# Stick-breaking attention: sums over later keys as fp32r products of a high and a low part, three units per head pair in place of four

## The reference, cut to what matters

```python
z = jnp.einsum('bhqd,bhkd->bhqk', q_blk, kt).astype(jnp.float32) * scale
mask = key_pos[None, :] < q_pos[:, None]
log_not = jnp.where(mask, jax.nn.log_sigmoid(-z), 0.0)
between = lax.cumsum(log_not, axis=3, reverse=True) - log_not
a = jnp.where(mask, jnp.exp(jax.nn.log_sigmoid(z) + between), 0.0)
return jnp.einsum('bhqk,bhkd->bhqd', a.astype(vt.dtype), vt)
```

## Time and profile before

| | |
|---|---|
| median of 3 runs | 2131.18 us (2130.68 to 2132.56) |
| the profiled execution's own time | 2132.41 us |
| its span in the trace | 2130.7 us |
| PE busy | 2027.6 us (95%) |
| DVE, ACT, POOL busy | 1144.8, 858.7, 341.2 us |
| mean granted clock of PE | 0.982 |
| attention stage, first matmul to last copy | 891.5 to 1015.9 us |
| PE, DVE, ACT, POOL busy in 891 to 1012 us | 106.7, 54.8, 68.9, 49.8 us |

### The profile page before, as it was taken

How to read it: one execution, slowest core, us unless ns; L and a number is a source line. 1 busy time by engine, 2 the same in 40 slices (tenths; PEclk the granted TensorE clock), 3 DMA queues, 4 the chain that set the end, 5 groups by cost and what they waited for, 6 DMA issues and landing times. The chain is left out here.

```text
span 2130.7 us, 27982 instructions
## 1 busy us (share of the span) xinstructions
PE 2027.6 (95%) x11430; PEld 1603.4 (75%) x11430; DVE 1144.8 (54%) x1422; ACT 858.7 (40%) x1242; POOL 341.2 (16%) x310
## 2 busy tenths in 40 slices
PE   8999889899988989998999999999999999999998
PEld 5777886577787768744778888877889878888886
DVE  4445537644564753244468547635332967745753
ACT  4246424524543451355345324333123735423432
POOL 1200615120062520144220000022000012000002
PEclk9999989999998999999999999999999999999999
DMA  6211102221111222200222232223322012223221
GB/s 231 73 66 40 42 18 103 106 73 60 40 42 50 71 86 92 100 30 0 79 99 81 93 113 91 83 94 125 112 79 80 1 60 81 98 90 117 98 83 67
DMA packets 30787, 167.64 MB, mean 79 GB/s; under 512 B 2827, under 2 KB 9635, under 8 KB 14916
## 3 DMA queue, kind: packets, MB, share of 16 engines
q1 hardware_dynamic: 30228, 165.07, 22.3%
q10 hardware_dynamic: 432, 0.79, 0.1%
HBM read 159.52 MB, written 10.00 MB: 80 GB/s over the span
## 5 line engine op out<-in xcount | busy, mean ns | idle before, releaser
L305 PE MATMUL psum<-inputs_high,weights_high 128*128 128x512 f32 x928 | 384.4, 414 | 24.3 <-DVE inputs_low L253 16.6
L307 PE MATMUL psum<-inputs_high,weights_low 128*128 128x512 f32 x928 | 368.2, 397 | 0.0
L306 PE MATMUL psum<-inputs_low,weights_high 128*128 128x512 f32 x928 | 367.8, 396 | 0.0
L2098 PE MATMUL psum<-inputs_high,weights_high 128*128 128x512 f32 x704 | 276.2, 392 | 0.5 <-DVE inputs_low L2242 0.5
L2100 PE MATMUL psum<-inputs_high,weights_low 128*128 128x512 f32 x704 | 274.0, 389 | 0.0
L2099 PE MATMUL psum<-inputs_low,weights_high 128*128 128x512 f32 x704 | 274.0, 389 | 0.0
L258 DVE TENSOR_TENSOR weights_low<-weights_raw,weights_high 128x2048 fp32r<-128x2048 f32 x68 | 160.3, 2359 | 190.1 <-ACT weights_high L247 190.0
L305 PEld LDWEIGHTS psum<-inputs_high,weights_high 128*128 128x128 f32 x928 | 176.3, 190 | 82.3 <-DVE inputs_low L253 22.0
L306 PEld LDWEIGHTS psum<-inputs_low,weights_high 128*128 128x128 f32 x928 | 176.8, 190 | 41.5 <-issue 5.3
L247 ACT CAST weights_high<-weights_raw 128x2048 fp32r<-128x2048 f32 x68 | 129.0, 1898 | 195.2 <-PE psum L307 179.8
L307 PEld LDWEIGHTS psum<-inputs_high,weights_low 128*128 128x128 f32 x928 | 176.5, 190 | 40.5
(11 more groups left out here) (384 smaller groups left out, 3220.5 us busy)
## 6 DMA issues: line engine op xcount, KB each, us to landing
weights_raw<-w_stream SPq DMA_DIRECT2D x116, 1024.0 KB, 4.8
weights_raw<-w_down SPq DMA_DIRECT2D x32, 704.0 KB, 4.0
residual_parked<-residual SPq DMA_DIRECT2D x2, 2048.0 KB, 10.1
residual_back<-residual_parked SPq DMA_DIRECT2D x2, 2048.0 KB, 7.8
residual<-x_t SPq DMA_DIRECT2D x2, 1024.0 KB, 7.8
bias_by_row<-bias_rows SPq DMA_DIRECT2D x2, 1024.0 KB
bias_by_row<-bias_rows SPq DMA_DIRECT2D x1, 1536.0 KB
out_t<-residual SPq DMA_DIRECT2D x5, 256.0 KB, 2.4
```

What stands on the lines that cost most here:

```text
L305: pe.matmul(out, hi, self.ahi[:, k], start=start and b == 0, stop=False)
L306: pe.matmul(out, hi, self.alo[:, k], start=False, stop=False)
L307: mm = pe.matmul(out, lo, self.ahi[:, k], start=False, stop=stop and b == blocks - 1)
L2098: pe.matmul(out, wh, hi, start=start, stop=False)
```

## The change

The unit list goes from four to three per pair. Unit n=0 holds key tiles 3 and 2 side by side (128 and 256 queries), n=1 holds tile 1 (384), and n=2 holds tile 0 (512); the widths with both heads are 768, 768 and 1024 columns. POOL no longer keeps a running total: it copies softplus to a high part with fp32r as its result (into the buffer `weights_high`, which is free in this stage), and DVE subtracts to make the low part (into `weights_low`). PE sums anew for each key tile: the triangle over the tile's own high and low parts, and minus ones over the parts of every later tile, with fp32r operands. The table of minus ones and the triangle is copied to fp32r once. DVE's list is now `softplus(u)`, `cap(u+2)`, `low(u)`, and PE's triangle products wait for `low(u)`.

```diff
...
-    negtri, negones = con[:, K_NEGTRI:K_NEGTRI + P], con[:, K_NEGONES:K_NEGONES + P]
-    pairs = SB_HEADS // 2
-    units = [(p, jt) for p in range(pairs) for jt in reversed(range(TT))]
+    pairs, per = SB_HEADS // 2, 3
+    units = [(p, n) for p in range(pairs) for n in range(per)]
...
-    with ExitStack() as stack, phase(nc, "z", "capped", "exp", "log", "softplus", "masked", "later", "sums", "weights",
-                                     "kept", "out", "out_copy", "bias_repeated") as s:
+    width = (3 * P, 3 * P, 4 * P)
+    blocks = (((3, 0, P), (2, P, 3 * P)), ((1, 0, 3 * P),), ((0, 0, 4 * P),))
+    earlier = (((0, 0, P, 2 * P),),
+               ((0, P, 3 * P, P), (0, 0, P, 2 * P)),
+               ((1, 0, 3 * P, P), (0, P, 3 * P, 2 * P), (0, 0, P, 3 * P)))
+    with ExitStack() as stack, phase(nc, "z", "capped", "exp", "log", "softplus", "masked", "high", "low", "sums", "weights",
+                                     "kept", "out", "out_copy", "signs", "bias_repeated") as s:
...
-        later = stack.enter_context(sbuf(nc, "later_keys", [P, 2, 2, T], F32))
...
+        signs = stack.enter_context(sbuf(nc, "minus_ones", [P, 2 * P], F32R))
+        negtri, negones = signs[:, 0:P], signs[:, P:2 * P]
+        parts = [x.rearrange("p u c -> p (u c)") for x in (k.whi, k.wlo)]
...
         def zbank(u):
...
-        def made_later(u):
-            return (TT - 1) * (u // TT) + min(u % TT, TT - 1)
+        def part(x, p, n):
+            first = 2 * 3 * P * (2 * n + p % 2 if n < 2 else 4)
+            return x[:, first:first + 2 * width[n]].rearrange("p (y i) -> p y i", y=2)
...
             @block.tensor
             def _(pe):
                 def scores(u):
-                    p, jt = units[u]
+                    p, n = units[u]
                     if u >= 3:
...
+                    for m, (jt, first, end) in enumerate(blocks[n]):
+                        for y in range(2):
+                            rows = slice(64 * y, 64 * y + 64)
+                            mm = pe.matmul(zbank(u)[:, y, first:end], qk[rows, 8 + p, jt * P:(jt + 1) * P],
+                                           qk[rows, p, jt * P:], start=m == 0, stop=False, skip_group_check=True)
+                    mm.then_inc(s.z, 1)
+                def sums(u):
+                    p, n = units[u]
+                    if n == 0:
+                        pe.wait_ge(s.low, u + 1)
+                    else:
+                        pe.wait_ge(s.softplus, u + 1)
+                    for of, first, end, to in earlier[n]:
+                        for y in range(2):
+                            for x in parts:
+                                pe.matmul(zbank(u)[:, y, to:to + end - first], negones, part(x, p, of)[:, y, first:end],
+                                          start=False, stop=False, skip_group_check=True)
+                    if n:
+                        pe.wait_ge(s.low, u + 1)
                     for y in range(2):
-                        rows = slice(64 * y, 64 * y + 64)
-                        mm = pe.matmul(zbank(u)[:, y, jt * P:], qk[rows, 8 + p, jt * P:(jt + 1) * P],
-                                       qk[rows, p, jt * P:], start=True, stop=False, skip_group_check=True)
-                    mm.then_inc(s.z, 1)
-                def sums(u):
-                    p, jt = units[u]
-                    pe.wait_ge(s.softplus, u + 1)
-                    pe.wait_ge(s.masked, u + 1)
-                    if jt < TT - 1:
-                        pe.wait_ge(s.later, 2 * made_later(u))
-                    for y in range(2):
-                        if jt < TT - 1:
-                            pe.matmul(zbank(u)[:, y, (jt + 1) * P:], negones, later[:, u % 2, y, (jt + 1) * P:],
-                                      start=False, stop=False, skip_group_check=True)
-                        mm = pe.matmul(zbank(u)[:, y, jt * P:], negtri, softp[:, u % 2, y, jt * P:],
+                        pe.matmul(zbank(u)[:, y, 0:width[n]], negtri, part(parts[0], p, n)[:, y],
+                                  start=False, stop=False, skip_group_check=True)
+                        mm = pe.matmul(zbank(u)[:, y, 0:width[n]], negtri, part(parts[1], p, n)[:, y],
...
                 def values(u):
-                    p, jt = units[u]
+                    p, n = units[u]
...
-                    if jt == TT - 1 and p >= 2:
+                    if n == 0 and p >= 2:
...
-                    for y in range(2):
-                        hd = 2 * p + y
-                        mm = pe.matmul(ps[64 * y:64 * y + 64, 6 + p % 2, jt * P:], v[:, jt, hd * 64:hd * 64 + 64],
-                                       w[:, u % 2, y, jt * P:], start=jt == TT - 1, stop=jt == 0,
-                                       skip_group_check=True)
+                    for jt, first, end in blocks[n]:
+                        for y in range(2):
+                            hd = 2 * p + y
+                            mm = pe.matmul(ps[64 * y:64 * y + 64, 6 + p % 2, jt * P:], v[:, jt, hd * 64:hd * 64 + 64],
+                                           w[:, u % 2, y, first:end], start=jt == TT - 1, stop=jt == 0,
+                                           skip_group_check=True)
...
                 for u in range(3):
                     scores(u)
+                pe.wait_ge(s.signs, 1)
                 for u in range(n_units + 1):
                     if u < n_units:
                         sums(u)
...
             @block.vector
             def _(dve):
                 def cap(u):
-                    jt = units[u][1]
+                    n = units[u][1]
...
                     if u >= 3:
...
-                    dve.tensor_scalar(zc[:, u % 3, :, jt * P:], zbank(u)[:, :, jt * P:], 40.0, None, ALU.min) \
+                    dve.tensor_scalar(zc[:, u % 3, :, 0:width[n]], zbank(u)[:, :, 0:width[n]], 40.0, None, ALU.min) \
...
                 def softplus(u):
-                    jt = units[u][1]
+                    n = units[u][1]
...
                     if u >= 2:
-                        dve.wait_ge(s.sums, u - 1)
-                        dve.wait_ge(s.later, 2 * made_later(u - 1))
-                    dve.tensor_tensor(softp[:, u % 2, :, jt * P:], zbank(u)[:, :, jt * P:], zc[:, u % 3, :, jt * P:],
-                                      ALU.max).then_inc(s.softplus, 1)
+                        dve.wait_ge(s.high, u - 1)
+                        dve.wait_ge(s.low, u - 1)
+                    dve.tensor_tensor(softp[:, u % 2, :, 0:width[n]], zbank(u)[:, :, 0:width[n]],
+                                      zc[:, u % 3, :, 0:width[n]], ALU.max).then_inc(s.softplus, 1)
+                def low(u):
+                    p, n = units[u]
+                    dve.wait_ge(s.high, u + 1)
+                    dve.tensor_tensor(part(parts[1], p, n), softp[:, u % 2, :, 0:width[n]],
+                                      part(parts[0], p, n).bitcast(F32), ALU.subtract).then_inc(s.low, 1)
...
                 def copy_out(p):
-                    dve.wait_ge(s.out, TT * (p + 1))
+                    dve.wait_ge(s.out, per * (p + 1))
...
+                dve.tensor_copy(signs[:], con[:, K_NEGTRI:K_NEGTRI + 2 * P]).then_inc(s.signs, 1)
                 cap(0)
                 cap(1)
                 for u in range(n_units):
                     softplus(u)
                     if u + 2 < n_units:
                         cap(u + 2)
-                    if u >= 5 and (u - 5) % TT == 0:
-                        copy_out((u - 5) // TT)
+                    low(u)
+                    if u >= per + 1 and (u - per - 1) % per == 0:
+                        copy_out((u - per - 1) // per)
...
             def _(act):
                 def logs(u):
-                    jt = units[u][1]
-                    z = zc[:, u % 3, :, jt * P:]
+                    z = zc[:, u % 3, :, 0:width[units[u][1]]]
...
                 def weights(u):
-                    jt = units[u][1]
+                    n = units[u][1]
...
                     if u >= 2:
...
-                    act.activation(w[:, u % 2, :, jt * P:], zbank(u)[:, :, jt * P:], ACT.Exp).then_inc(s.weights, 1)
+                    act.activation(w[:, u % 2, :, 0:width[n]], zbank(u)[:, :, 0:width[n]], ACT.Exp).then_inc(s.weights, 1)
                 for u in range(n_units + 1):
                     if u < n_units:
                         logs(u)
...
             @block.gpsimd
             def _(pool):
-                def keep(x, jt):
-                    d = x[:, :, jt * P:(jt + 1) * P]
+                def keep(x, n):
+                    tiles = len(blocks[n])
+                    d = x[:, :, 0:tiles * P].rearrange("p y (b i) -> p y b i", b=tiles)
...
-                                              pattern=[[0, 2], [1, P]], channel_multiplier=-1)
+                                              pattern=[[0, 2], [0, tiles], [1, P]], channel_multiplier=-1)
                 for u in range(n_units + 1):
                     if u < n_units:
```

(20 more changed lines are left out.)

## The result

The changed kernel takes 2151.42 us (median of 4 runs, 2148.96 to 2155.24) against 2131.87 for the one before in the same comparison (median of 4, 2130.68 to 2135.4): 19.5 us more, ratio 1.009 (95% interval 1.0076 to 1.0103). I had forecast 9.6 us more, with a range of 2133 to 2153.

What follows compares the result with a forecast made beforehand. Bound: a ring of sums, weights and scores, PE and ACT taking turns. Seven pairs 4.5 plus start and end 3.1 made 7.6, plus clock 2: +9.6 us, from 2131.2 to 2141; range 2133 to 2153.

Steps and rivals of the forecast that it cites:

- The ring: Attention stage, every unit: low, sums, weights, scores, cap, next low; 15.88 us per pair against 15.24, seven pairs 4.5 us more.
- the narrow products: Four minus-ones products of 128 columns behind low at n = 0: priced 0.84 us; from below 0.116 each, 0.46.
- The parts off the ring: Ones products, softplus and POOL's copy beside the ring: hidden, with only 0.3 us to spare at n = 2.
- Start and end: Attention stage outside its seven pairs of ring: 7.3 and 13.5 us against 17.7 before, 3.1 us more.
- The clock: Half PE speed over one or two units, at the stage's start and end: 2 us more, bounds 0 and 4.
- If PEclk falls in mid-stage: Sign that the prediction is wrong: PE's granted clock falling in the middle of the attention stage; no size given.
- The half-clock rival: Much slower: PE at half clock throughout the attention stage, +40 us, about 2181; chance 0.08.
- the port rival: Slower: DVE and POOL hold each other up, each low waiting for one keep; 1.5 us more per pair, 2153; chance 0.10.
- The faster rival: The old ring still binds, cap and low staying off it: 12.8 us per pair, about 2115; chance 0.06.

Runs made afterwards that it cites:

- Low twice: The changed kernel with every low done twice, one behind the other with a wait between: 2188.2 us, ratio 1.0265 to the kernel before.
- the two other orders of DVE: The changed kernel with DVE's list reordered: low(u) ahead of cap(u+2), 2137.35 us; or cap(u+1) in place of cap(u+2) ahead of low(u), 2118.57 us.
- the filler: The changed kernel plus 8 fp32r products of zeros on PE before the sums of each pair's first unit: 2139.46 us, ratio 1.0032 to the kernel before.
- the orders with low right behind POOL: The changed kernel with low(u) ahead of cap(u+2), 2137.35 us, or with cap(u+1) ahead of low(u), 2118.57 us; in both low waited for POOL's high.
- the order with cap one unit ahead: The changed kernel with DVE's list as softplus(u), cap(u+1), low(u): 2118.57 us, ratio 0.9955 to the kernel before.
- low before cap: The changed kernel with DVE's list as softplus(u), low(u), cap(u+2): 2137.35 us, ratio 1.0023 to the kernel before.

## Why the prediction was right and wrong

*The ring.* Right in place; in size too, but in part by luck, since the price of the narrow products and the rest of the ring were off in opposite ways. 7 pairs at 15.80 instead of 15.24 make 3.9 us; the prediction had 4.5. Low twice and the two other orders of DVE show that it is this order that sets the pace. The parts off the ring were hidden as said (ones, softplus, POOL's copy at 0.82 and 1.04 us).

*The narrow products.* Wrong in the value chosen: they start 0.11 to 0.12 us apart, as the lower bound had it. The Trainium skill, page "TensorE: Matmul & The Clock Gate", section "Back-to-back issue gap", gives about 81 ns at 128 columns; this trace has 110 to 120, so the measurement decides.

*Start and end.* The prediction had 3.1 us more. With the filler it is 131.92 - 7 x 15.80 = 21.3 us instead of 17.7: 3.6. Of this 0.5 us is the first round and the round with the wide low of 1.36, which are longer than 15.80; cut as the prediction cuts it, from the stage's start to the first low's end and from the last pair's first low's end to the end, it is 7.3 and 13.5 us, just as forecast.

*The clock.* This is the step that failed: "I add 2 (bounds 0 and 4)". The clock came to 11.1 us, the difference of the stages with and without filler. The mechanism was named, as half clock after PE's gaps, but placed at the start and the end alone. There the price was about right: 2.9 us in the first round and 0.1 at the end. What failed is that the six rounds between were put at nothing, where the runs showed 8.1 us: five of the six had half clock after the gap of 2.2 us in which PE waits for low. "If PEclk falls in mid-stage" stood among the signs of being wrong, and it did. The half-clock rival was turned down with "no idle stretch in the ring reaches the 4 us" of the earlier trace rows. That argument failed twice. The 4 us were the time between two windows of one gap, which lasted 5.98 us, and not a least length; the gap in the ring is 2.2 us, behind a stretch that PE filled only in part, and half clock followed it in most pairs but not in all (the pair from 950.43 kept 2.4 GHz). And I had set only full speed throughout against half speed throughout, while the case that came lies between: one stretch in most pairs. Stage by parts: 3.9 + 3.6 + 11.1 = 18.6 of 18.65 us. That 2151.42 us still lies inside the range of 2133 to 2153 is luck: the upper end was drawn for the port rival, not for the clock.

The span grew 2 us less than the stage: 0.4 us by an earlier start, and the rest in the output product behind it. There the kernel before ran some 3.4 us at half clock, and the changed one none. Six microseconds of that product, before and after (PEclk is the third value from the end):

```profile
1020.00:1026.00 6.00, 4.85 (x14) 3.88 (x15) 6.00 (x10) 4.04 (x6) 0.00 (x0) 0.72 0.52 178
```

```profile
1038.00:1044.00 6.00, 4.63 (x20) 3.87 (x21) 6.00 (x10) 4.27 (x6) 0.00 (x0) 1.00 0.52 175
```

What selects the pairs that lose their clock was not settled; the filler shows only that it depends on PE's work in the gap. The medians moved 19.5 us and this one span 16.6. The difference is the spread of single runs: the profiled execution of the changed kernel took 2148.96 us, 2.5 under its median, and that of the kernel before 2132.41, 0.5 over the median beside it.

*The port.* In the changed kernel it counted little: two wide lows of 1.35 and 1.41 us, where the others took 1.22, show it. Once it went the other way: a select of 512 columns that started 0.19 us after a low (1023.02, low at 1022.83) took 1.27 us in place of 0.64, and low kept its 0.96. In the orders with low right behind POOL it was plain. The rule in the Trainium skill, page "SBUF — State Buffer", section "Who interferes with whom", agrees: low, which reads two SBUF tensors, was drawn out beside a select and was not once the select came later. How long it is held is not quite as the rule has it: of the selects 0.33 and 0.55 us were left when low was due (0.42 and 0.64 less 0.09), and low grew by 0.20 and 0.41, 0.13 or 0.14 less.

*The faster rival.* Its sum for a pair with cap and low off the ring, 12.8 us, is what the order with cap one unit ahead took. Whether that kernel runs by the terms of that sum was not looked into.

## What to carry to other kernels

When an instruction is added to an engine's hand-written list, look at what stands ahead of it and how old a unit that one waits for: the same change cost 19.5 us with low behind the cap of unit u+2, and gained 12 with low behind the cap of unit u+1. When a ring gets longer gaps of PE, price the clock in every round, as a case between never and always, and test it with filler work, which costs one edit. Shorter matmuls alone did not help here: with low behind the cap of unit u+2, a pair of fp32r sums took 15.80 us at full clock, one of plain sums in the same three units 15.17. With low behind a cap one unit older it took 12.8.

## What the runs showed of the hardware

- fp32r products of 128 columns started 0.11 to 0.12 us apart, of 256 columns 0.12, of 384 columns 0.17 and of 512 columns 0.23; so from 256 columns down to 128 nothing was gained (changed kernel, 951.4 to 962.4 us).
- In the changed kernel PE's granted clock fell from 1.00 to 0.50 (2.4 to 1.2 GHz) in or after the gap of 2.2 us in five of the six middle rounds, stayed there for 3.4 us four times and 6.8 once, and did not fall in any of these rounds once zero products filled the gap.
- A DVE subtraction of 768 columns with two SBUF inputs took 0.95 us alone, and 1.15 or 1.36 us when it started 0.09 us after a POOL select of 0.42 or 0.64 us had begun (low before cap); with the select held back until low was done it took 0.96.
